# A two-layer diffusion trunk step: half-width copies in the triangular inverse's levels, the last sums written as rows, one copy less in the scan

## What is computed

```python
def gdn_scan(q, k, v, log_alpha, beta, S0):                      # gated delta rule, chunked
    A = jnp.where(strict, bc[..., :, None] * kk * decay, 0.0)
    sol = lax.linalg.triangular_solve(jnp.eye(CHUNK) + A, rhs, left_side=True, lower=True)
    ...
def block(args):                                                 # in peer(); per token 128 experts ib of 16384
    act = jax.nn.gelu(jnp.einsum('ted,td->te', jnp.take(u_tab, ib, axis=0), xb), approximate=False)
    return jnp.einsum('te,ted->td', gb * act, jnp.take(v_tab, ib, axis=0))
def trunk_layer(x, ...):
    ...                                                          # norm, four mixers, projection
    x = x + g1 * y
    x = x + g2 * peer(h2, ...)                                   # g2: one number per column of x
```

## Time and profile before

| | |
|---|---|
| runs | 2714.13, 2720.18, 2713.28 us; median 2714.13 |
| profiled execution | 2716.72 us; span from first to last instruction 2714.9 us |
| busy share of the span | PE 66%, PE weight load 40%, DVE 61%, ACT 14%, POOL 54% |
| granted TensorE clock, mean | 0.82 |
| DMA | 959.36 MB, 353 GB/s over the span; 805.40 MB of it gathered rows |

### The profile page before, as it was taken

One profiled execution on the slowest core, in us unless ns is written; L12 is line 12 of the kernel. 1 busy time (PEld: TensorE's weight loads), 2 busy tenths in 40 slices (PEclk: granted clock), 3 DMA queues, 4 the chain that ended last, 5 costly groups with the idle time before them and its releaser, 6 DMA issues. The chain is left out here.

```text
span 2714.9 us, 28087 instructions
## 1 busy us (share of the span) xinstructions
PE 1781.1 (66%) x10274; PEld 1092.8 (40%) x10274; DVE 1645.7 (61%) x4093; ACT 380.4 (14%) x903; POOL 1454.9 (54%) x1540
## 2 busy tenths in 40 slices
PE   6988688768984111089888797768992000088888
PEld 5857567646634011053253386655650000011112
DVE  2526898871589998941117389882299999900000
ACT  3222231211112000011111132112110000000000
POOL 0000553342666676767765444333566777777775
PEclk9989698868996555599999898778996555599999
DMA  9487796666999999999999897656999999999998
GB/s 399 162 341 294 285 405 215 204 229 227 400 410 420 420 420 420 420 374 416 400 421 419 316 380 290 205 198 239 347 410 381 420 420 420 420 420 420 392 419 338
DMA packets 249208, 959.36 MB, mean 353 GB/s; under 512 B 32368, under 2 KB 33648, under 8 KB 231280
## 3 DMA queue, kind: packets, MB, share of 16 engines
q0 software_dynamic: 221184, 805.40, 74.9%
q1 hardware_dynamic: 19584, 142.62, 13.1%
q10 hardware_dynamic: 8304, 9.56, 1.0%
HBM read 955.11 MB, written 2.36 MB: 353 GB/s over the span
## 5 line engine op out<-in xcount | busy, mean ns | idle before, releaser
L542 POOL DMA_INDIRECT sb_ring<-in_peer_u,sb_idxu x768 | 726.7, 946 | 773.1 <-DVE sb_idxT L1939 287.2
L542 POOL DMA_INDIRECT sb_ring<-in_peer_v,sb_idxT x768 | 728.0, 948 | 463.9 <-issue 212.2
L1971 DVE CUSTOM_DVE_ANT_0 sb_ring<-sb_ring,pv 128x1024 f32<-128x1024 f32 x768 | 906.9, 1217 | 32.5 <-DMA sb_ring<-in_peer_u,sb_idxu 26.0
L565 PE MATMUL pv<-sb_ring,sb_wcol 128*32 128x512 f32 x3072 | 646.5, 617 | 73.9 <-DMA sb_ring<-in_peer_v,sb_idxT 64.8
L565 PE MATMUL pb<-sb_hT,sb_wring 128*128 128x256 f32 (+1 forms) x1920 | 379.5, 358 | 49.5 <-ACT sb_big L1092 27.1
L565 PEld LDWEIGHTS pb<-sb_hT,sb_wring 128*128 128x128 f32 x1920 | 324.7, 205 | 124.4 <-issue 70.9
L565 PEld LDWEIGHTS pv<-sb_ring,sb_wcol 128*32 128x32 f32 x3072 | 125.0, 111 | 540.7 <-DMA sb_ring<-in_peer_v,sb_idxT 365.8
L568 PE MATMUL pb<-sb_cst,sb_dots 128*128 128x128 f32 x6 | 2.6, 426 | 417.6 <-DVE sb_dots L1977 417.6
L565 PE MATMUL pb<-sb_big 128*128 128x128 f32 (+2 forms) x1888 | 241.5, 292 | 32.5 <-DVE sb_big L1654 22.7
L565 PEld LDWEIGHTS pb<-sb_big 128*128 128x128 f32 (+1 forms) x1888 | 229.9, 202 | 54.3 <-DVE sb_big L1654 29.7
L1985 DVE COPY sb_accv<-pv 128x512 f32<-128x512 f32 x12 | 8.3, 689 | 342.6 <-PE pv L565 338.1
(11 more groups left out here) (234 smaller groups left out, 1656.9 us busy)
## 6 DMA issues: line engine op xcount, KB each, us to landing
sb_ring<-in_w_mod_blocks SPq DMA_DIRECT2D x38, 1024.0 KB, 8.3
sb_wring<-in_w_in_blocks SPq DMA_DIRECT2D x34, 1024.0 KB, 7.8
sb_wring<-in_w_q_blocks SPq DMA_DIRECT2D x26, 1024.0 KB, 8.6
sb_wring<-in_w_out_blocks SPq DMA_DIRECT2D x14, 1024.0 KB, 7.8
sb_ring<-in_peer_u,sb_idxu POOLq DMA_INDIRECT x768, 9.1
sb_ring<-in_peer_v,sb_idxT POOLq DMA_INDIRECT x768, 8.0
sb_wring<-in_w_mod_blocks SPq DMA_DIRECT2D x10, 1024.0 KB, 7.5
sb_ring<-in_w_in_blocks SPq DMA_DIRECT2D x6, 1024.0 KB, 17.4
```

The lines of the kernel that those rows point to most:

```text
L542: pool.indirect_dma_start(ring[:, j, :], None, a["tab_" + kind][l_of(q)], bass.IndirectOffsetOnAxis(ap=of, axis=0)).then_inc(rows_in[j], 16)
L565: return nc.tensor.matmul(out, lhsT, rhs, start=start, stop=stop)
L1971: dve.tensor_tensor_reduce(out=row, in0=row, in1=pv[:, :, :].rearrange("p a b -> p (a b)"), scale=1.0, scalar=0.0, op0=ALU.mult, op1=ALU.a ...
```

## The change

It has three parts.

**Half the columns.** At level lv only the columns with bit lv equal to d matter for P and X, and those with bit lv equal to 1 - d for XT. `bit_columns` selects them: runs of 2^lv columns, every second run. ACT's copy of P and DVE's two merges go over four heads by 64 columns instead of 128. A memset of 512 columns of `big` joins the start, since the other half of P is now never written in unit 0.

**The last unit's sums end as rows.** A row of g2 on all partitions is made once (`gaterow`: DVE multiplies the identity by g2 eight times, PE multiplies with ones, ACT copies). The three tiles of xT are transposed and copied to `big` ahead of time: the prompt's tile before the last u phases and its output DMA right away (`outrows`), the sample's behind it (`xrows`). After each of the last two v phases `item_last` multiplies each half of `pv` by `gaterow` and adds it to the row of x, and ACT sends each half (256 KB) off. `item_end` for q = 4 and 5 and `item_final`'s transposes are gone.

**The scan.** In the first of its two turns a product goes straight to `og` instead of to `tmp` and then by a copy (L1707) to `og`.

```diff
@@ schedule()
+    main += [("gaterow",), ("outrows", 0)]
     for q, t in seq_tiles(3):
         main.append(("u", q, t, 0, STEPS, (0, 1)))
+    main += [("xrows", 1), ("xrows", 2)]
     for q, t in seq_tiles(3):
-        main += [("gelu", q, t), ("v", q, t, 0, STEPS, (0, 1)), ("end", 3, q, t)]
+        main += [("gelu", q, t), ("v", q, t, 0, STEPS, (0, 1)), ("last", q, t)]
     main.append(("final",))
@@ helpers
+        gaterow = big[:, 0:D]
+        gatediag = hT[:, :, 0:P]
+        def xrow(t):
+            return big[:, D * (1 + t):D * (2 + t)]
+        def bit_columns(ap, lv, bit):
+            return ap.rearrange("p n (b two r) -> p n b two r", two=2, r=1 << lv)[:, :, :, bit, :]
+        def heads_of(bank):
+            return bank.rearrange("p (n j) -> p n j", n=4)
@@ PE, item_v
-                        pe.wait_ge(*done("v_summed", (q - 1, 1)))
+                        pe.wait_ge(*done("v_summed" if q < 5 else "y_row", (q - 1, 1)))
@@ ACT, st_intra
-                        fn(big_at(3072 + 512 * d, 512), pb[:, d, :]).then_inc(*tick("p_copied", (u, i, d, lv)))
+                        fn(bit_columns(big_at(3072 + 512 * d, 4, P), lv, d), bit_columns(heads_of(pb[:, d, :]), lv, d)) \
+                            .then_inc(*tick("p_copied", (u, i, d, lv)))
@@ ACT, items
+            def item_outrows(t):
+                item_xrows(t)
+                act.wait_ge(*done("x_out_copied", (t, 1)))
+                act.dma_start(outs["yp"][0], xrow(t)).then_inc(*tick("out_y", t, 16))
+            def item_last(q, t):
+                for k in range(2):
+                    act.wait_ge(*done("y_row", (q, k)))
+                    o = slice(512 * k, 512 * k + 512)
+                    act.dma_start(outs["ys"][0, (t - 1) * P:t * P, o], xrow(t)[:, o]).then_inc(*tick("out_y", (t, k), 16))
@@ DVE, st_intra
-                            dve.copy_predicated(x, bc1(lvl[:, 1 - d, lv, :], 4), pb[:, 2 + d, :].rearrange("p (a b) -> p a b", b=P)) \
+                            dve.copy_predicated(bit_columns(x, lv, d), bit_columns(bc1(lvl[:, 1 - d, lv, :], 4), lv, d),
+                                                bit_columns(heads_of(pb[:, 2 + d, :]), lv, d)) \
                                 .then_inc(*tick("x_ready", (u, i, d, lv)))
@@ DVE, st_scan
-                            tt(heads_by_parity(tmp.rearrange(h4, h=4)),
+                            part = og[:, i, :] if turn == 0 else tmp
+                            tt(heads_by_parity(part.rearrange(h4, h=4)),
...
-                                dve.tensor_copy(og[:, i, :], tmp).then_inc(*step())
-                                dve.wait_ge(*stepped())
@@ DVE, items
+            def item_gaterow():
+                for j in range(DC):
+                    last = ts(gatediag[:, j, :], ident, modT[:, 1, 40 + j, 1:2], None, ALU.mult)
+                last.then_inc(*tick("gate_diag"))
+            def item_last(q, t):
+                dve.wait_ge(*used(rows_before(phase_of["v", q]) + SLOTS - 1))
+                dve.wait_ge(*done("gaterow_copied", 1))
...
+                for k in range(2):
+                    dve.wait_ge(*done("x_out_copied", (t, k)))
+                    o = slice(512 * k, 512 * k + 512)
+                    scaled = big_at(4 * D + 512 * k, 512)
+                    tt(scaled, pv[:, k, :], gaterow[:, o], ALU.mult).then_inc(*step())
+                    dve.wait_ge(*stepped())
+                    tt(xrow(t)[:, o], xrow(t)[:, o], scaled, ALU.add).then_inc(*tick("y_row", (q, k)))
```

More of the change, by code:

```diff
@@ L1083, in _ @@
             gap, run = engine_schedule({"const": item_const, "modquad": item_modquad, "samplerows": item_samplerows, "gelu": item_gelu,
[L1084 removed]
+                                        "v": item_v, "end": item_end, "gaterow": item_gaterow, "xrows": item_xrows,
+                                        "outrows": item_outrows}, stages)
             run()
@@ L1461, in _ @@
                                         "samplerows": item_samplerows, "gelu": item_gelu, "v": item_v,
+                                        "gaterow": item_gaterow, "xrows": item_xrows, "outrows": item_outrows, "last": item_last,
                                         "final": item_final}, stages)
@@ L1999, in _ @@
             gap, run = engine_schedule({"const": item_const, "modsum": item_modsum, "u": item_u, "gelu": item_gelu,
-                                        "end": item_end}, stages)
+                                        "end": item_end, "gaterow": item_gaterow, "last": item_last}, stages)
             run()
```

54 lines of the change are left out of this document (33 added, 21 removed).

## The result

The changed kernel takes 2673.45 us (median of four runs, 2670.96 to 2678.63) against 2717.15 us (2713.28 to 2721.01): ratio 0.9846, 95% interval 0.9818 to 0.9873, 35 to 49 us less. Two later comparisons of the same kernels gave 0.9867 (0.9847 to 0.9888) and 0.9857 (0.9832 to 0.9882).

The account below looks back on a forecast made before the run. No engine bounds the whole span: DVE paces the inverse in units 1 and 3, gathered rows the last 650 us. Gains 18.4 + 0.3 + 1.3 + 0.5 + 7.7 less 1.0 give 27.2 us: median 2687 us, range 2676 to 2701.

Parts of the forecast that it names:

- Merges: DVE's merges in the inverse of units 1 and 3: 267 ns less each, 19 and 14 on the path per unit.
- rival B: Inverse of units 1 and 3: part of the gain given back to PE or full gather stages, 2695 to 2703 us; chance 0.17.
- rivals C and D: C: halves take as long as wholes, 2705.6 us, chance 0.07. D: strided access slower, 2741 us, chance 0.02.
- term of 18.4 us: Inverse of units 1 and 3: shorter merges plus each tile's last copy of P, 9.2 us per unit.
- Rival E: More gain: merges save 361 ns each, unit 2 gives some, the clock stays up; 2670 to 2679 us, chance 0.08.
- Copies: ACT's copy of P, 597 to 383 ns: hidden within levels, only a tile's last one counts, 0.21 us.
- Units 0 and 2: Their inverses: unit 0 PE bound, gains 0.3 us; unit 2 bound by PE and gathers, gains 0.
- Scan: Four copies of 321 ns leave DVE's own chain: 1.3 us gained.
- End: From DVE's last start of sums to the span's end: 5.6 us instead of 13.3, 7.7 us gained.
- Output DMAs: Prompt's and first sample tile's outputs travel among gathers that fill the queues: 1.0 us lost, bounds 0 to 2.5.
- Preparation: `gaterow`, `outrows`, `xrows` around the last u phases: cost 0, or 2.15 us were the slack gone.
- Hand-over: From v of q = 4 to v of q = 5: 0.5 us gained, POOL's stall 4.4 us, clock effect put at 0.

Follow-up runs that it names:

- filler_end: Kernel before plus eight extra 128x128 matmuls in PE's pause in the last two levels of the first tile of units 1 and 3: 0.9929 of the kernel before.
- no_half3: Changed kernel with copies and merges at full width again, third try, at 420 GB/s: 0.9949 of the kernel before.
- half_only3: Kernel before with the half-width copies and merges alone, third try, at 420 GB/s: 0.9898 of the kernel before.
- gelu_early2: Changed kernel with the last gelu moved ahead of the last but one sum of rows, second try: 0.9866 of the kernel before.
- after_again: The changed kernel, unaltered, measured a second time: 0.9867 of the kernel before.
- after_third: The changed kernel, unaltered, measured a third time: 0.9857 of the kernel before.

## Why the prediction was right or wrong

**Merges: right in sum.** I took 267 ns a merge; from level 2 on it is 277 ns (0.61 to 0.335 us from start to start), at level 1 only 40 to 90. The levels of the first tile fell from 39.39 and 40.18 to 34.00 us and of the second from 37.07 to 33.26: 19.2 us over four tiles, against the 18.4 of the sum. PE did not become the bound (5.89 us a level against the 5.93 forecast, VectorE without a pause), so rival B fell; rivals C and D fell with the 0.42 us, though at level 1 a piece of C came true. The merges were to be equal at all levels by the forecast: those of level 1 are not (0.71 to 0.76 us), those of level 2 are. On "SBUF — State Buffer" of the Trainium skill, section "Specifications (TRN2)", I had leaned for runs of two; this case's 0.73 us does not agree with a free run of two for a predicated copy, and does agree for a plain one, 0.42.

**The step that failed** is the term of 18.4 us for the half widths. It prices VectorE's merges and ScalarE's last copy alone and leaves PE's matmuls behind the levels as long as they were. The same stretches gave 25.7 us. The merges themselves were sized well: with the clock up, the levels are 39.17 us long at full widths (filler_end) and 34.00 at half in a first tile, 37.07 and 33.26 in a second, 17.9 us in all. The clock was put at nothing: 1.2 us are the last levels of units 1 and 3, which had run partly at half clock before (39.39 and 40.18 us), and 3.6 are the stretches from the last merge to the first copy (3.77 to 2.09, 3.76 to 2.09, 2.38 to 2.09), at the upper clock instead of the lower. These 4.9 us are shown. The remaining 2.9 lie between the stretches, where behind the first tiles the clock had stayed at half for 13.7 and 17.1 us in all before and stays there for 3.4 to 6.8 us now; how much of them is the clock and how much what executions differ by stays open. That a shorter mix moves all later gathers forward held: POOL issued the first row of the last u phases at 2049.2 and 2047.2 us with full widths, and at 2020.4, 2020.1, 2017.9 and 2011.9 us with half widths.

The trace of before had shown it: the 45 us of unit 3 in the earlier trace rows stand at a clock of 0.92, and I read from the same row only that VectorE was the bound. Most of the 0.08 below 1 was the last six microseconds, at 0.59. I had weighed the clock at one place, the hand-over, and not where the change shortened a pause. Rival E had "the clock stays up" among three causes, at a chance of 0.08, and the first median, 2673.45 us, lies in its range. Of its causes only that one came true: the merges saved 277 and not 361 ns, and unit 2 gave nothing. The rest of the way into that range is luck of the first four runs, as told under the frame below.

**Copies.** Hidden while the merges are full, as said; once they are short, hidden and 4 to 6 us are not told apart. A copy takes 386 ns, against the 383 forecast.

**Units 0 and 2.** As forecast: from the first merge to the last 35.76 us in unit 0 (36.04 before, the 0.3 of the sum), and in unit 2 57.6, 58.3 and 59.0 us in the three profiles of the changed kernel (58.0 before, 59.2 in no_half3). From the span's start to unit 1's start it is 261.1 to 266.6 us at 420 GB/s, in kernels of both kinds without order.

**Scan.** Forecast 1.3. From the second tile's copy to the end of the scan it is 58.6, 57.7, 58.8 and 58.8 us with the copy and 57.1 or 57.2 in the three profiles of the changed kernel, but 58.3 and 57.1 in no_half3, which has no copy either. Over two units that is 116.3 and 117.6 us with the copy and 114.3 to 115.4 without, 1 to 3 us; filler_end, with the copy, has 115.4 as well. So the 1.3 are neither shown nor refuted.

**End.** 13.3 to 5.2 us: 8.1 against 7.7. Right; and half_only3, with the old end, has 12.9. At the end, where no gathers are left, the 512 KB landed 2.60 us after their issue and the 256 KB land after 2.02, so halving a transfer saves a few tenths, as the prediction's estimate had it. (The section that it draws on is about DMAs that GpSimd issues; these are ScalarE's, and the two figures make their fixed part 1.4 us, an estimate, not 2.)

**Output DMAs.** Forecast a loss of 1.0. From the first row of the last u phases to the first of the last v phase it is 479.7, 478.6 and 479.0 us in three kernels with the old end and 480.0, 480.8 and 480.6 in the three profiles of the changed one: 1.4 us. Right in size. It fits the prompt's 512 KB, which go out 16 to 17.5 us after the first row: VectorE starts the 61st row 8.0, 8.7 and 8.4 us after POOL issued it, where it was 7.6, 6.5 and 7.0, and PE's first matmul of the v phase of q = 4 comes 13.0, 14.0 and 13.6 us after that phase's first issue, where it came after 12.9, 11.7 and 12.2. The sample's two halves go out after the last v phase's first row and are not in this stretch.

**Preparation.** Forecast 0. From the first row of the last u phases to the first of the v phases it is 318.2, 318.0 and 318.1 us, against 318.0 in the three kernels with the old end.

**Hand-over.** PE starts 4.99 instead of 5.63 us after VectorE, 0.6 us against 0.5, and POOL's stall is 4.00 against the 4.4 forecast. What I got wrong is what it is worth: the stretch behind it is 1.4 us shorter, which fits that the DMA queue had run empty in the stall before and no longer does, and the further 2.1 us of gelu_early2 arrived nowhere. PE started the phase at 0.59 and 0.55 of the clock, as before at 0.51.

**Both together.** From the first row of the last u phases to PE's last matmul it was 652.3, 651.4 and 651.9 us with the old end and is 651.2, 652.6 and 651.7 us: what the output DMA costs and what the hand-over gives cancel. The forecast had a loss of 0.5 us.

**The frame.** The first medians lie 44 us apart, those of the later comparisons give 36 and 39 us, and the three intervals overlap. So some 5 to 8 of the 44 us are best read as luck of the first four runs. With the half widths at 25.7 the forecast's own sum would be 34.5 us.

## What to carry to other kernels

A granted clock a little below 1 over a long stretch is the mean of two levels: find the microseconds at half, look at the pause ahead of them, and when a change shortens that pause, price the matmuls behind it at the upper level, and give the lower level a chance of its own. Shortening the engine that the matmuls wait for then pays twice; extra matmuls in the pause can buy the second part alone, but only where the pause is longer than they are. A stall of the engine that issues transfers cost nothing here as long as the queue behind it stayed full, and cost once it ran empty (DMA share 1.03 in one kernel's stall, 0.21 at the end of the other's): read the DMA share in the stall and just behind it before pricing it.

## What the runs showed of the hardware

**Equal pauses, different clock.** The attention stages of units 1 and 3 took 62.9 to 63.7 us in some executions and 67.1 to 72.1 in others, on chips at 420 GB/s, in kernels of both kinds. Stretches from the middle of unit 3's attention in after_again:

```profile
1837.00:1847.00 10.00, 8.77 (x41) 8.21 (x40) 0.42 (x1) 2.80 (x6) 1.99 (x3) 0.50 0.72 279
1847.00:1857.00 10.00, 9.82 (x37) 8.42 (x38) 0.97 (x2) 0.18 (x2) 0.00 (x0) 0.80 0.00 0
```

and in gelu_early2, whose instructions are the same there:

```profile
1833.00:1843.00 10.00, 8.43 (x57) 7.65 (x57) 0.79 (x2) 2.47 (x6) 2.28 (x3) 1.00 0.74 294
1843.00:1853.00 10.00, 10.00 (x51) 8.53 (x53) 1.09 (x4) 0.00 (x0) 0.00 (x0) 1.00 0.29 105
```

The six transposes ahead of this waited 1.70 us for the same work in both, and the clock fell in one only. Each such place is worth up to 7 us, which is as large as much of what was argued over here. Of the three profiled executions of the changed kernel the one with a short stage (after_third, 63.6 us in unit 1) has a span 8 and 9 us below the other two, about 6 of them in that stage. That the rest of the spread among runs of one kernel (2669.8 to 2686.2 us for the changed one) comes from the same is likely but not shown. Whether filler_end's fill made the short form likelier (two of two stages, against three of eighteen in the other nine profiles at that rate) stays open.

**Predicated copies.** With an output in runs of one or two fp32 of every two or four, `copy_predicated` of 128x256 takes 0.72 to 0.73 us instead of 0.43 to 0.45; a mask or a PSUM source in runs of two costs nothing (0.44), and a plain copy with the same output is not slowed (0.42).

**Chips.** The same program took 2717 us on some chips and 2907 to 2925 on others, which read the gathered rows at 370 instead of 420 GB/s; there the half widths alone gave 17 and 21 us instead of 28.
